# Token-major residual and 512-column output projections in a two-block diffusion transformer

## What is computed

```python
# first block
x = x + ga1 * mlstm_mixer(modulate(x, g_mix, sh1, sc1), modulate(ctx, ...))   # "lstm"
x = x + ga2 * conv_glu(modulate(x, g_ffn, sh2, sc2))                          # "f0", 2816 hidden
x = rmsnorm(x, g_final)                                                       # "fin"
# second block
def sublayer(x, shift, scale, gate, g_pre, g_post, fn, w):
    h = rmsnorm(x, g_pre) * (1 + scale) + shift
    return x + w * gate * rmsnorm(fn(h), g_post)
# layer 0: f1 = swiglu, gla = gated linear attention, f2 = swiglu
# kv = shared keys and values, from rmsnorm(x after f2)
# layer 1: f3 = swiglu, mla = latent attention, f4 = swiglu
```

## Time and profile before

| what | us |
|---|---|
| three runs | 1564.87, 1570.95, 1577.61 |
| median | 1570.95 |
| span of the profiled execution | 1557.6 |
| PE busy | 1455.5 |

### The profile page before, as it was taken

One profiled execution on the slowest core, in us unless ns is written; L12 is line 12 of the kernel. 1 busy time (PEld: TensorE's weight loads), 2 busy tenths in 40 slices (PEclk: granted clock), 3 DMA queues, 4 the chain that ended last, 5 costly groups with the idle time before them and its releaser, 6 DMA issues.

```text
span 1557.6 us, 28387 instructions
## 1 busy us (share of the span) xinstructions
PE 1455.5 (93%) x10962; PEld 1397.8 (90%) x10962; DVE 1073.6 (69%) x1458; ACT 716.2 (46%) x934; POOL 102.7 (7%) x198
## 2 busy tenths in 40 slices
PE   6899989999989999999989999899999977899997
PEld 4888878999989999988889999799999876799996
DVE  5786695887767777678667886667786764555542
ACT  6514435555355443455455443454435543554432
POOL 0011000000100110100001110001100000000000
PEclk9999998999999999999999999999999989999998
DMA  8577232777866888856437887758976430255550
GB/s 346 228 252 248 95 109 71 266 257 243 291 235 210 320 292 296 300 184 220 150 112 280 304 317 279 250 178 308 335 274 241 149 135 28 84 213 173 182 187 27
DMA packets 60726, 337.58 MB, mean 217 GB/s; under 512 B 6880, under 2 KB 7264, under 8 KB 32112
## 3 DMA queue, kind: packets, MB, share of 16 engines
q1 hardware_dynamic: 32544, 234.67, 41.7%
q0 software_dynamic: 27936, 101.72, 19.2%
q10 hardware_dynamic: 176, 0.16, 0.0%
HBM read 335.49 MB, written 1.05 MB: 216 GB/s over the span
## 4 chain that ended last, share of the span: by engine, by line
PE 78%; DVE 10%; DMA 4%; ACT 4%; issue 2%; DVEq 0%; POOLq 0%; POOL 0%; SPq 0%; ACTq 0%
PE bank L194 22%; PE bank L195 22%; PE bank L196 22%; PE bank L199 12%; DMA mring<-m_stream 4%; DVE wlo L188 3%; DVE mring L351 1%; ACT whi L182 1%; DVE T L324 1%; DMA raw<-w_stream 1%; DVE hlo L329 1%; ACT lnt L287 0%; ACT SQ L272 0%; DVE T L399 0%; DVE mx L1734 0%
## 5 line engine op out<-in xcount | busy, mean ns | idle before, releaser
L194 PE MATMUL bank<-hhi,whi 128*128 128x256 f32 x2280 | 651.7, 286 | 26.4 <-DVE hlo L329 19.4
L195 PE MATMUL bank<-hlo,whi 128*128 128x256 f32 x2280 | 646.7, 284 | 0.0
L196 PE MATMUL bank<-hhi,wlo 128*128 128x256 f32 x2280 | 646.5, 284 | 0.0
L188 DVE TENSOR_TENSOR wlo<-raw,whi 128x2048 fp32r<-128x2048 f32 x219 | 500.6, 2288 | 159.2 <-ACT whi L182 155.9
L182 ACT ACTIVATE whi<-raw 128x2048 fp32r<-128x2048 f32 x219 | 417.6, 1909 | 259.3 <-PE bank L196 222.8
L194 PEld LDWEIGHTS bank<-hhi,whi 128*128 128x128 f32 x2280 | 438.9, 192 | 32.8 <-issue 24.0
L195 PEld LDWEIGHTS bank<-hlo,whi 128*128 128x128 f32 x2280 | 439.3, 193 | 0.3
L196 PEld LDWEIGHTS bank<-hhi,wlo 128*128 128x128 f32 x2280 | 439.1, 193 | 0.0
L351 DVE SCALAR_TENSOR_TENSOR mring<-mring,cb 128x1024 f32<-128x1024 f32 x192 | 233.7, 1221 | 133.3 <-DMA mring<-m_stream 133.0
L195 PE MATMUL bank<-hid_lo,whi 128*128 (+1 forms) x880 | 249.0, 283 | 0.0
L196 PE MATMUL bank<-hid_hi,wlo 128*128 (+1 forms) x880 | 248.6, 282 | 0.0
(11 more groups left out here) (233 smaller groups left out, 1142.1 us busy)
## 6 DMA issues: line engine op xcount, KB each, us to landing
raw<-w_stream SPq DMA_DIRECT2D x219, 1024.0 KB, 6.4
mring<-m_stream POOLq DMA_DIRECT2D x192, 512.0 KB, 5.1
con<-const_d SPq DMA_DIRECT2D x1, 1472.0 KB, 10.4
X<-xT SPq DMA_DIRECT2D x1, 1024.0 KB, 11.4
XC<-ctxT SPq DMA_DIRECT2D x1, 1024.0 KB, 9.4
cb<-c_row POOLq DMA_DIRECT2D x2, 512.0 KB, 5.3
y<-X SPq DMA_DIRECT2D x1, 1024.0 KB, 3.9
cols<-cols_d SPq DMA_DIRECT2D x1, 222.5 KB, 7.4
```

The lines of the kernel that those rows point to most:

```text
L188: nc.vector.tensor_tensor(wlo[:, c % 3], raw[:, c % 3], whi[:, c % 3].bitcast(f32), ALU.subtract).then_inc(s_lo, 1)
L194: nc.tensor.matmul(out, wh, rhi, start=start, stop=True, skip_group_check=True)
L195: nc.tensor.matmul(out, wh, rlo, start=False, stop=True, skip_group_check=True)
L196: return nc.tensor.matmul(out, wl, rhi, start=False, stop=True, skip_group_check=True)
```

## The change

- `X` is token-major: `X[:, t]` holds 128 tokens (token tile t) by 1024 features. The last projection of every stage takes the activations as the stationary operand (128 tokens of one input tile) and 512 weight columns as the moving one. Its four groups (token tile t, half h) lie in banks 0 to 3. A chunk takes 24 matmuls. In the last chunk alone the groups are finished one after the other (`pe_out_last`).
- Norms of rows: ACT squares 512 columns with an accumulator, a one-column addition, a logarithm and an exponential of one column (`act_row_rstd`). The statistics on PE are gone between stages.
- The next input is made by a float32 matmul of `X[:, t]` with a diagonal matrix of the reciprocal roots (`dg`), which scales and transposes at once (`pe_pre`); DVE applies scale and shift from PSUM, ACT rounds, DVE takes the rest.
- The gate is wanted along the free axis: `act_gate_row` writes it as a column to DRAM and loads it back as a row on all partitions, on ACT's queue, during the stage.
- `raw`, `whi`: four slots; `wlo` is written in place over `raw`. SP therefore loads chunk c only when PE has used chunk c-4. Up projections have four banks.
- kv's input is made at the start of f3 (same transposed `X`); its products stay between f3 and mla, with the transpositions of mla's input between them.
- All hardware loops are written out. At the start, the weights are stationary and c has 4 columns; `xT` is loaded into `XF` and transposed by PE.
- `X` goes out by token tile: transposed, copied to `OUT` by DVE and ACT, four transfers.

```diff
-        raw = sb("raw", [P, 3, CW])
-        whi = sb("whi", [P, 3, CW], f32r)
-        wlo = sb("wlo", [P, 3, CW], f32r)
+        raw = sb("raw", [P, SLOTS, CW])
+        raw_at = nc.sbuf_base - SLOTS * CW * 4
+        wlo = nc.alloc_sbuf_tensor_at("wlo", [P, SLOTS, CW], f32r, offset=raw_at)
+        whi = sb("whi", [P, SLOTS, CW], f32r)
...
-                    sp.wait_ge(s_lo, c - 2)
-                    sp.dma_start(raw[:, c % 3], w_stream[c]).then_inc(s_raw[c % 3], 16)
+                    if c >= SLOTS:
+                        sp.wait_ge(s_pe, c - SLOTS + 1)
+                    sp.dma_start(raw[:, c % SLOTS], w_stream[c]).then_inc(s_raw[c % SLOTS], 16)
...
+        def mm3w(out, c, w, hi, lo, start):
+
+            wh, wl = whi[:, c % SLOTS, w:w + 512], wlo[:, c % SLOTS, w:w + 512]
+            mm(out, hi, wh, start)
+            mm(out, hi, wl, False)
+            return mm(out, lo, wh, False)
...
+        def pe_out_last(pe, chunks, k0, hi, lo, mid=None):
+
+            for i, (t, h) in enumerate(GROUPS):
+                if i == 3 and mid is not None:
+                    mid()
+                for n, c in enumerate(chunks):
+                    for g in range(2):
+                        k = k0 + 2 * n + g
+                        ins = mm3w(out_bank(t, h), c, g * D + h * 512, tok(hi, k, t), tok(lo, k, t), False)
...
+        def act_row_rstd(act, n, src, wait, out=False, between=None):
+
+            for h in range(2):
+                act.wait_ge(*wait(h))
+                ins = nc.scalar.activation(junk[:], src(h), ACT.Square, accum_out=ss[:, n, h:h + 1])
...
+                if h == 0:
+                    alink(act, nc.scalar.activation(uu[:, n:n + 1], ss[:, n, 0:1], ACT.Identity, bias=eps[:, 0:1],
+                                                    scale=1.0 / D))
+                    if between is not None:
+                        between()
+            alink(act, nc.scalar.activation(rl[:, n:n + 1], ss[:, n, 1:2], ACT.Ln, bias=uu[:, n:n + 1], scale=1.0 / D))
+            nc.scalar.activation(rr[:, n:n + 1], rl[:, n:n + 1], ACT.Exp, scale=-0.5).then_inc(s_rr, 1)
...
+        def act_boundary(act, stage):
...
+            for t in range(2):
+                if stage not in PLAIN:
+                    act_row_rstd(act, rn("post", stage, t), lambda h: out_bank(t, h),
+                                 lambda h: out_ready(stage, t, h), True,
+                                 (lambda: act_pre(act, pre, 0)) if t and pre else None)
...
+                if pre:
+                    act_row_rstd(act, rn("pre", pre, t), lambda h: xrow(t, h), lambda h: (s_xu, x0 + h + 1))
+                    if t or stage in PLAIN:
+                        act_pre(act, pre, t)
...
+        def dve_boundary(dve, stage):
+
+            pre = NEXT[stage]
+            for t in range(2):
+                dve_product(dve, stage, t, 0)
+                if t and pre:
+                    dve_pre_split(dve, pre, 0)
+                dve_product(dve, stage, t, 1)
+                dve_update(dve, stage, t)
+                if pre:
+                    dve_pre(dve, pre, t)
...
+            if pre:
+                dve_pre_split(dve, pre, 1)
+            if pre == "f3":
+                for t in range(2):
+                    dve_pre_split(dve, "kv", t)
...
+            pe_out_last(pe, (c0 + FT + last,), 2 * last, hid_hi, hid_lo)
+            pe_pre(pe, pre, 0)
```

More of the change, by code:

```diff
@@ L30 @@
 N_UNITS = N_MOD - FIRST_MODS
+SLOTS = 4
+STAGES = ["lstm", "f0", "f1", "gla", "f2", "f3", "mla", "f4"]
+NEXT = dict(zip(STAGES, ["f0", "f1", "gla", "f2", "f3", "mla", "f4", None]))
+PLAIN = ("lstm", "f0")
+ROW_NORMS = []
+for _s in STAGES:
+    for _t in range(2):
+        ROW_NORMS += [] if _s in PLAIN else [("post", _s, _t)]
+        ROW_NORMS += [("fin", _s, _t)] if _s == "f0" else []
+        ROW_NORMS += [("pre", NEXT[_s], _t)] if NEXT[_s] else []
 _names = [("g_mix", 8), ("g_ffn", 8), ("g_final", 8), ("gain", 8), ("cw0", FT), ("cw1", FT), ("cw2", FT),
@@ L313, in build, with dve_modulate @@
         s_t = sem("input_tile_scaled")
[L315 to L317 removed]
+        MODULATED, _n = {}, 0
+        for _name in ("x1", "ctx", "f0", "f1", "gla", "f2", "f3", "kv", "mla", "f4"):
+            MODULATED[_name] = _n
+            _n += 8 if _name in ("x1", "ctx") else 4 if _name == "kv" else 10
+        def dve_modulate(dve, n, A, sh, stage, src, hi=hhi, lo=hlo):
             u0 = U[stage]
@@ new lines, in build, with rn, xrow, turned @@
+        for _s in STAGES:
+            XU[_s] = _n
+            _n += 8 if _s == "f0" else 4
+        OUT_LAST = {"lstm": C_LSTM + 16, "gla": C_GLA + 16, "mla": C_MLA + 7}
+        for _f in range(5):
+            OUT_LAST[f"f{_f}"] = C_FFN[_f] + FFN_CHUNKS - 1
+        def rn(kind, stage, t):
+            return ROW_NORMS.index((kind, stage, t))
+        def xrow(t, h):
+            return X[:, t, h * 512:(h + 1) * 512]
+        def turned(t, b):
+            return bank[(6, 7, 0, 1)[2 * t + b]]
@@ new lines, in four, with act_pre @@
+        def four(x):
+            return x.rearrange("p (a b) -> p a b", a=4)
+        def act_pre(act, name, t):
+            hi = khi if name == "kv" else hhi
+            t0 = MODULATED[name] + 2 * t
+            if t == 0 or name == "kv":
+                for b in range(2):
+                    act.wait_ge(s_t, t0 + b + 1)
+                    nc.scalar.activation(hi[:, 4 * b:4 * b + 4, t * P:(t + 1) * P], TX[:, 4 * b:4 * b + 4],
+                                         ACT.Copy).then_inc(s_hhi, 1)
+            else:
+                for j in range(DT):
+                    act.wait_ge(s_t, t0 + j + 1)
+                    nc.scalar.activation(tok(hi, j, 1), TX[:, j], ACT.Copy).then_inc(s_hhi, 1)
@@ new lines, in act_ffn @@
+                act_split(act, c0 + t + 3)
+                act.wait_ge(s_prod, FT * f + t + 1)
+                nc.scalar.activation(hid_hi[:, t], T[:, t % 3], ACT.Copy).then_inc(s_hidhi, 1)
+                rows(t)
+            for d in range(FT // 2 - 1):
+                act_split(act, c0 + FT + d + 3)
+                if d in after:
+                    after[d]()
+        UP_UNITS = [0] + [1, 1, 2] * 7
+        UP_UNITS_0 = [0, 1, 1, 2] + [1, 0, 1] * 6
+        DOWN_UNITS = [0, 0] + [1, 1, 2] * 3
@@ L563, in dve_ffn @@
-            down_parts(dn, dve, after)
+                    rest(t - 1)
+                mods(n - min(n, 1))
+                after_up(t)
+            rest(FT - 1)
+            for d in range(FT // 2):
+                dve_split(dve, c0 + FT + d + 2)
+                mods((DOWN_UNITS if f else DOWN_UNITS_0)[d])
+                if d in after:
+                    after[d]()
         s_in = [sem(f"inputs_loaded{j}") for j in range(8)]
@@ L801, in act_lstm @@
             act_modulate(act, lambda j: modc[:, j:j + 1], "ctx", chi)
+            act.wait_ge(s_xt, 1)
+            for t in range(2):
+                nc.scalar.activation(xrow(t, 1), out_bank(t, 1), ACT.Copy).then_inc(s_xc, 1)
             act_split(act, c + 3)
```

779 lines of the change are left out of this document (430 added, 349 removed).

## The result

The changed kernel takes 1643.99 us (median of five runs, 1631.06 to 1644.47), the kernel before 1570.95: a ratio of 1.0466, 95% interval 1.0410 to 1.0523. The forecast was 1588, with a range up to 1606. The sign was right, the size wrong by 56. The profiled execution (time 1631.06) has a span of 1629.3; 71.7 more than the one before.

What follows compares the result with a forecast made beforehand. Matmul time on PE plus gaps without stage products bound the kernel. Gaps and f3's start +27.3, chunks -11.8, slips +2.0, start -0.5: +17.0 us, giving 1588 on the median; range 1558 to 1606.

Steps and rivals of the forecast that it cites:

- What bounds the kernel: Whole kernel: matmul time plus places where PE has no stage product; faster matmuls pay in full, gaps by their own chain.
- "-0.5" for the start: Start: 1.7 us of copies and turns go, 16 transpositions of XF (1.8) come; -0.5, between -2 and +3.
- The gap's chain: Between stages: with an output norm, next stage's first product at F+14.5 us, plus 1.5 for PE's lower clock.
- F: Moment when DVE is free for the gap: 4.0 us past the last product after f1 and f3, 5.5 after f2.
- Rival C: Weight stream: loads landing after 10 hold DVE and PE, 0.1 us in each of 165 feed-forward chunks, 1604 us; chance 0.15.
- f3 to mla: From f3's last product to mla's first: 39.8 us, against 31.5 and one statistic of 3.3 before; +5.0.
- Down chunks: Down projections: 55 chunks with matmuls at 0.234 us instead of 0.240 a pair, saving 8.1 us.
- out chunks: Out projections: 12 chunks fed from hhi at 0.227 us a matmul, saving 0.312 a chunk, 3.7 us.
- Hidden, with slips: +2: Weights in the steady state: load, ACT and DVE fit the three chunk times, 16.3 us; +2, between 0 and +10.
- the gate row's two transfers ... 0: Gate row inside stages: four up steps, 23 us, lie between its two transfers, so it costs 0.
- The end: End of the kernel: no splits or units; 10 us against 14.8, -4.8.
- rival A: Gaps hidden as meant, PE keeps its clock: gap after f0 +4.2, whole kernel 1546 us, faster; chance 0.15.

Runs made afterwards that it cites:

- e1: Changed kernel with the first modulation products back in their old form (padded c stationary, 512 weight columns moving): 1612.31 us, ratio 1.0289.
- e8: Kernel before with only the narrow first modulation products (weights stationary, four columns of c moving): 1595.38 us, ratio 1.0213.
- e4_filler: Changed kernel with 32 unread 512-column products ahead of each transposition after f0, f1, f2 and the first after f3: 1628.01 us, ratio 1.0392.
- e3: Changed kernel with the twelve conditioning units of a down projection moved forward, none in the last step: 1628.66 us, ratio 1.0390.
- e5: Changed kernel with five slots for raw weights and their rest and three for the rounded part, instead of four and four: 1640.75 us, ratio 1.0490.
- e6: Changed kernel with the output gate's row stored as 128 pieces of 32 bytes, read by DVE with a stride: 1638.22 us, ratio 1.0448.
- e12: Changed kernel with the feed-forward gate row turned on PE, stored as eight rows of 512 bytes, its transfers one up step later: 1619.56 us, ratio 1.0337.
- e17: Changed kernel with the first kv pair ahead of both turns of mla's input: 1644.50 us, ratio 1.0511.
- e9: Changed kernel with one 512-column product behind every fourth narrow product of the first modulation, 64 in all: 1661.65 us, ratio 1.0598.

## Why the prediction was wrong, point by point

- **What bounds the kernel: right.** Matmuls pay in full, and a gap by its own chain.
- **"-0.5" for the start: the step that failed, 26 of 55 us.** I counted the copies and turns that go and the 16 turns of `XF` that come (they take 1.9, priced at 1.8), and gave the new form of the first products no term at all. The diff had it in plain sight: 64 products of 512 columns became 256 with a weight load each. The earlier trace rows hold no price for such a product, but bounds were to be had: 256 x 0.120 = 31 us at the pitch of the earlier trace rows and twice that at the lower level, against 64 x 0.234 = 15. e1 and e8 show +25 in the traces, 26 and 30 in the medians, from both sides.
- **The gap's chain: right in its steps, 18.6 behind F instead of 16.0.** From F, DVE's first product (704.35), the diagonal of tile 0 was predicted at +4.15 and came at +4.4. Tile 0's second rounding ended at +10.4 instead of +8.0, tile 1's root at +14.8 instead of +12.35, the next stage's first product at +18.6 instead of +16.0 (14.5 and 1.5 for the clock). Two terms make 1.6 of the 2.6: each turn's first half 2.2 instead of 0.9 (709.07 to 711.26), since PE was at its lower level both times (the windows above, 0.57 and 0.54), so 2.6 where I had taken the middle, 1.5; and four scalings 1.37 instead of 0.9, since a scaling with two columns as operands takes 0.405, and I had priced it by the copy of the earlier trace rows. The rest is handovers. The fill of e4_filler makes the part behind F 2.0 to 2.2 shorter. The Trainium skill's rule ("TensorE: Matmul & The Clock Gate", section "HAM oscillation") wanted all of 2.8, as the prediction worked it out; the trace agrees with it (PE idle for 8.6 and 6.8 us before the two turns), and my middle value was unfounded.
- **F: T+3.9 after f1 (predicted +4.0), T+4.9 after f3 (+4.0), T+2.7 after f2 (+5.5).** With other runs at 2.3 to 4.8 after f1, the hit there is partly luck. The gap after f2 is luck as a whole: +6.8 against +6.7, from an F 2.8 too early and a chain 2.8 too long. e3 confirms that the units made most of F. Whether the ring of four slots had a part in it, as the prediction says, e5 leaves open. Rival C named the mechanism inside the stages, loads that land after 10 and hold DVE and PE; it didn't name what makes them late, which e6 and e12 show. Its size, 0.1 us a chunk, was nearly the loss: 15.4 us in 132 chunks.
- **f3 to mla: +5.0 predicted, +10.5.** About half is the turns: the second kv pair ends at 1299.85, T+27.6, where the walk had 25. The other half comes behind it: DVE finishes mla's input at 1298.4; then come kv's statistics and root, the latent, and behind the latent on DVE the split of the keys' weights:
```profile
1298.03 0.64 ACT L322 ACTIVATE SQL<-bank 128x256 f32<-128x256 f32 x2
...
1301.87 0.88 DVE L1694 SCALAR_TENSOR_TENSOR T<-bank,cols,rstd 128x256 f32<-128x256 f32 x2 [3.42 <-ACT rstd L340]
...
1303.57 2.29 DVE L213 TENSOR_TENSOR wlo<-raw,whi 128x2048 fp32r<-128x2048 f32 x1
```
  The keys start at 1305.9, 6.1 after the pair's end; my walk had 3.5 there, since I had not followed that split. e17 shows that PE's order is not the cause. That the split costs this is read from the trace only: to put it ahead of the latent, in DVE's idle 3.42, wasn't tried. The gap after lstm (+9.4) and those after gla and mla carry the mis-sized turns.
- **Down chunks: too small; out chunks: too large.** 54 steps of hid products, from 1594.62 to 1606.98, are 0.229 each, not 0.234.
```profile
1594.62 0.39 PE L224 MATMUL bank<-wlo,hid_hi 128*128 128x512 f32 x1
...
1606.98 0.39 PE L224 MATMUL bank<-wlo,hid_hi 128*128 128x512 f32 x1
```
  That saves 24 x (0.240 - 0.229) = 0.26 a chunk, 14.6 in 55, where I had 8.1; f4, which has no waits, is 2.8 shorter, as 11 chunks should make it. The products fed from hhi, which I had at 0.227, take 0.234 in this kernel, and those with chi 0.229: the operands have changed places since the earlier trace rows, so the arena doesn't explain it, and what does stays open. The 12 out chunks save 1.7 instead of 3.7. The Trainium skill's 216 ns at 512 columns ("TensorE: Matmul & The Clock Gate", section "Back-to-back issue gap") is not reached here: the trace disagrees by 13 to 18 ns.
- **"Hidden, with slips: +2" and "the gate row's two transfers ... 0": failed.** PE waits 15.4 us for weights in f0 to f3. I had looked at whether the row arrives in time, not at what its 1040 packets do to the streams beside them. e12 makes these stages 12.6 shorter. Of the 3.3 that stay, 3.0 is the wait for f3's third chunk, priced at +1.8: its split is ready 15.0 after f3's first product in the changed kernel, not 13.3, and PE waits 3.2.
- **The end: -2.7 instead of -4.8.** Shorter, as forecast, 12.0 where the walk had 10.
- **Slips in the sums.** A chunk time of 5.45, behind T-10.9 and 16.3, goes with 0.227, not with the 0.234 of the down chunks (0.3 us in F); and rival A's gap after f0 should read +3.7, not +4.2. Neither changes the forecast.

Together: 26 + 20 + 9 = 55 of missed time, and the edits that undo these causes bring back 84, since the order and the units also shorten what the prediction had counted.

## What to carry to other kernels

Give every changed loop in a diff a term of its own, also one that looks like a detail of the start; count its matmuls and its weight loads, and price them at both of PE's levels before one is taken. In a chain that alternates between engines for two tiles, write the queues of both engines out side by side: here the order alone was worth 20 us. And ask of every small transfer what it does to the large ones beside it.

## What the runs showed of the hardware

- A product with its own weight load costs 0.111 us at the upper and 0.213 at the lower level, with 4 columns as with 64.
- PE fell to its lower level at 53.7 us while it was busy without a pause, with narrow products; with one 512-column product in five among them the pitch stayed at the lower level (e9).
- The granted clock of the first stretch of a run reads 1.00 while the pitch is that of the lower level, with narrow products (0.213, until 42.6) and with wide ones (0.43, until 16 in e1).
- A 4 KB store in pieces of 4 bytes doubled the landing of 1 MB loads around it (11.7 against 5.1 us); beside stores in pieces of 32 or 512 bytes no load took over 10 us (e6, e12).
- The pitch of 512-column products at the upper level was 0.227 to 0.229 with some stationary operands and 0.234 us with others, and hhi and chi changed places between the two kernels.
- A DVE product of 512 columns whose second operand has a stride of eight elements takes 1.10 instead of 0.69 us.
